# Query heads store both products of the rotation; the key-value norm and the filler sums move with it

## The reference, cut to what matters

```python
proj = jnp.einsum("bsd,dp->bsp", u, w_in)          # q_lat (384), kv_lat (256), k_rope (32), ...
q = rms_norm(q_lat, q_norm_g) @ w_uq               # 8 heads of 64 + 32
q_nope, q_pe = jnp.split(q, [QK_NOPE], axis=-1)
q_pe = apply_rope(q_pe, cos, sin)                  # [x1*cos - x2*sin, x2*cos + x1*sin]
kv = rms_norm(kv_lat, kv_norm_g) @ w_ukv           # 8 heads of k_nope 64 + v 64
k_pe = apply_rope(k_rope, cos, sin)                # one for all heads
qf = concat(q_nope, q_pe);  kf = concat(k_nope, k_pe)
sc = einsum("bqhd,bkhd->bhqk", qb, k) * scale      # then mask, softmax, times v
```

## Time and profile before

| | us |
|---|---|
| median of 3 runs | 2353.86 |
| lowest, highest | 2351.16, 2355.52 |
| span of the profiled execution, first to last instruction | 2352.3 |
| busy in it: PE, DVE, POOL, ACT | 2254.0, 1487.5, 1082.5, 850.4 |
| mean granted TensorE clock (share of full speed) | 0.988 |

### The profile page before, as it was taken

The page is one execution under the profiler, slowest core; times in us unless marked ns, Lnnn a source line. Parts: engine busy times, 40 slices in busy tenths (PEclk is TensorE's granted clock), DMA queues, the critical chain, the costliest instruction groups (busy, mean ns, idle before and its releaser), DMA issues.

```text
span 2352.3 us, 29969 instructions
## 1 busy us (share of the span) xinstructions
PE 2254.0 (96%) x10766; PEld 1834.4 (78%) x10766; DVE 1487.5 (63%) x2357; ACT 850.4 (36%) x1387; POOL 1082.5 (46%) x1273
## 2 busy tenths in 40 slices
PE   6899999999999999999999999999999999999997
PEld 3688777788668877788867888887877878788886
DVE  5989866554478986765368776555775766533322
ACT  2443334222353333422245434344343444433321
POOL 1565436565446543666534455341444344443343
PEclk9999999999999999999999999999999999999999
DMA  8432224664243221354322223233244242222222
GB/s 307 134 110 82 68 73 143 207 202 156 72 143 108 81 67 59 130 169 149 116 81 73 92 99 104 79 116 119 85 123 138 90 126 77 71 72 72 72 81 72
DMA packets 93204, 259.80 MB, mean 110 GB/s; under 512 B 10129, under 2 KB 11537, under 8 KB 92945
## 3 DMA queue, kind: packets, MB, share of 16 engines
q1 hardware_dynamic: 71392, 210.23, 28.6%
q10 hardware_dynamic: 21680, 47.79, 5.7%
HBM read 237.01 MB, written 20.97 MB: 110 GB/s over the span
## 4 chain that ended last, share of the span: by engine, by line
PE 41%; issue 29%; POOL 19%; DVE 7%; ACT 2%; DMA 1%; POOLq 0%; ACTq 0%; DVEq 0%; SPq 0%
POOL t L422 19%; PE bank L2132 13%; PE bank L2133 13%; PE bank L2134 13%; DVE t L1786 3%; PE bank L2206 1%; DVE t L1224 1%; PE bank L2183 1%; DMA t<-blocks 1%; PE bank L2522 1%; DVE t L1228 0%; PE bank L2225 0%; DVE t L1783 0%; POOL t L432 0%; DVE t L1257 0%
## 5 line engine op out<-in xcount | busy, mean ns | idle before, releaser
L422 POOL TENSOR_TENSOR t<-t,t 128x256 fp32r<-128x256 f32 x1208 | 1030.5, 884 | 1179.4 <-ACT t L485 1178.9
L2132 PE MATMUL bank<-t,t 128*128 128x512 f32 (+1 forms) x3056 | 1175.4, 385 | 32.9 <-DVE t L1224 9.4
L2133 PE MATMUL bank<-t,t 128*128 128x512 f32 (+1 forms) x3056 | 1148.4, 376 | 0.0
L2134 PE MATMUL bank<-t,t 128*128 128x512 f32 (+1 forms) x3056 | 1147.2, 375 | 0.0
L2132 PEld LDWEIGHTS bank<-t,t 128*128 128x128 f32 x3056 | 580.0, 190 | 163.5 <-issue 16.0
L2133 PEld LDWEIGHTS bank<-t,t 128*128 128x128 f32 x3056 | 580.0, 190 | 103.2 <-issue 4.2
L2134 PEld LDWEIGHTS bank<-t,t 128*128 128x128 f32 x3056 | 578.4, 189 | 105.1
L485 ACT ACTIVATE t<-t 128x1024 fp32r<-128x1024 f32 x302 | 317.2, 1054 | 287.5 <-PE bank L2134 240.1
L1288 DVE SCALAR_TENSOR_TENSOR t<-t,t,t 128x512 f32<-128x512 f32 x168 | 156.4, 950 | 101.8 <-DMA t<-w_ada 62.0
L1571 DVE SCALAR_TENSOR_TENSOR t<-t,t,t 128x512 f32<-128x512 f32 x240 | 206.1, 859 | 6.7
L1228 DVE SCALAR_TENSOR_TENSOR t<-t,bank 128x512 f32<-128x512 f32 x112 | 76.7, 685 | 153.3 <-ACT t L1181 59.9
(11 more groups left out here) (251 smaller groups left out, 1731.2 us busy)
## 6 DMA issues: line engine op xcount, KB each, us to landing
t<-blocks SPq DMA_DIRECT2D x306, 512.0 KB, 3.6
t<-w_ada SPq DMA_DIRECT2D x144, 256.0 KB, 2.7
t<-w_ada SPq DMA_DIRECT2D x20, 512.0 KB, 11.6
xm_park<-t ACTq DMA_DIRECT2D x16, 384.0 KB, 2.3
s_park<-t ACTq DMA_DIRECT2D x16, 384.0 KB, 2.3
t<-xm_park ACTq DMA_DIRECT2D x16, 384.0 KB, 4.5
t<-s_park ACTq DMA_DIRECT2D x16, 384.0 KB, 5.0
xc_park<-t ACTq DMA_DIRECT2D x16, 256.0 KB, 2.3
```

The source lines that it names most:

```text
L422: low = pool.tensor_tensor(w_lo[slot][:, part], w_raw[slot][:, part], w_hi[slot][:, part].bitcast(F32), ALU.subtract)
L2132: pe.matmul(out, wh, xh, start=start, stop=False)
L2133: pe.matmul(out, wh, xl, start=False, stop=False)
L2134: return pe.matmul(out, wl, xh, start=False, stop=stop)
```

## The change

- `qf` and `kf` have 128 rows instead of 96. For a query head DVE makes one multiplication over rows 64 to 127 (bank times `rope`), straight into `qf`, with no temporary and no addition. The two products stand as separate rows, and the score's sum over 128 rows adds them; for that the rotated key stands in rows 64 to 95 and again in 96 to 127 of `kf`.
- For the key the two products are made as before; the sum is written twice. PE's head 3, which takes the key's bank, waits for the two products (`k_parts`) instead of for the sum.
- The key-value norm on DVE is placed behind head 0 instead of behind head 1, knH on ACT behind head 3 instead of head 5, knL on DVE behind head 4 instead of head 3.
- The steps of `products` are called behind heads 4 to 7 (`products(B_UQ + h // 2 + 1)`) instead of behind heads 0, 1, 3, 5 and 7. The order on SP, the table `ADA_AT` and the points of `split_to` on ACT stay as they are.
- The four filler sums ahead of head 6 on PE are gone, and the wait for `kv_std` with them.

```diff
-        qf, kf = at(R_Q, [96, HEADS, S]), at(R_Q + 16 * KB, [96, HEADS, S])
+        qf, kf = at(R_Q, [128, HEADS, S]), at(R_Q + 16 * KB, [128, HEADS, S])
...
                     if h in (2, 5):
                         split_to(B_UQ(l) + RING + (h + 1) * 3 // 8)
-                    if h == 5:
+                    if h == 3:
                         for j in range(2):
                             act.wait_ge(dve_done, Dn(l, "kn", j))
...
-                def rotate(dst, bank, *label):
+                def turned_keys(bank):
...
-                    dve.tensor_tensor(dst, tmp[3][64:96, :], tmp[4][64:96, :], ALU.add).then_inc(dve_done, d(*label))
+                    for half in (slice(64, 96), slice(96, 128)):
+                        dve.tensor_tensor(tmp[2][half, :], tmp[3][64:96, :], tmp[4][64:96, :], ALU.add).then_inc(dve_done, d())
+                    cd.also(l, "k_rope")
...
                 for h in range(HEADS):
                     wp(l, "q", h)
-                    rotate(qf[64:96, h, :], banks[Q_BANK[h % 4]], l, "q_pe", h)
+                    dve.tensor_tensor(qf[64:128, h, :], banks[Q_BANK[h % 4]][64:128, :], rope[64:128, :], ALU.mult).then_inc(dve_done, d(l, "q_pe", h))
                     if h == 0:
-                        products(B_UQ(l))
-                    if h == 1:
-                        products(B_UQ(l) + 1)
-
                         wa(l, "kv_std")
...
-                    if h == 3:
+                    if h == 4:
                         for j in range(2):
                             wa(l, "knH", j)
                             low(knL[:, j, :], kv_lat[:, j, :], knH[:, j, :], l, "knL", j)
-                    if h % 2:
+                    if h >= 4:
                         products(B_UQ(l) + h // 2 + 1)
...
-                    if h == 6:
-                        pe.wait_ge(act_done, A(l, "kv_std"))
-                        keep_busy(2, 4)
...
-                        pe.wait_ge(dve_done, Dn(l, "k_rope"))
+                        pe.wait_ge(dve_done, Dn(l, "k_parts"))
```

More of the change, by code:

```diff
@@ L1487, in _ @@
                 products(B_KR(l))
-                def rotate(dst, bank, *label):
+                def turned_keys(bank):
                     wd()
                     dve.tensor_tensor(tmp[3][64:96, :], bank[64:96, :], rope[64:96, :], ALU.mult).then_inc(dve_done, d())
-                    dve.tensor_tensor(tmp[4][64:96, :], bank[96:128, :], rope[96:128, :], ALU.mult).then_inc(dve_done, d())
+                    dve.tensor_tensor(tmp[4][64:96, :], bank[96:128, :], rope[96:128, :], ALU.mult).then_inc(dve_done, d(l, "k_parts"))
                     wd()
-                    dve.tensor_tensor(dst, tmp[3][64:96, :], tmp[4][64:96, :], ALU.add).then_inc(dve_done, d(*label))
+                    for half in (slice(64, 96), slice(96, 128)):
+                        dve.tensor_tensor(tmp[2][half, :], tmp[3][64:96, :], tmp[4][64:96, :], ALU.add).then_inc(dve_done, d())
+                    cd.also(l, "k_rope")
                 wp(l, "k_rope")
-                rotate(tmp[2][64:96, :], banks[1], l, "k_rope")
+                turned_keys(banks[1])
                 for h in range(HEADS):
                     wp(l, "q", h)
-                    rotate(qf[64:96, h, :], banks[Q_BANK[h % 4]], l, "q_pe", h)
+                    dve.tensor_tensor(qf[64:128, h, :], banks[Q_BANK[h % 4]][64:128, :], rope[64:128, :], ALU.mult).then_inc(dve_done, d(l, "q_pe", h))
                     if h == 0:
-                        products(B_UQ(l))
-                    if h == 1:
-                        products(B_UQ(l) + 1)
                         wa(l, "kv_std")
@@ L1517, in _ @@
                             low(knL[:, j, :], kv_lat[:, j, :], knH[:, j, :], l, "knL", j)
-                    if h % 2:
+                    if h >= 4:
                         products(B_UQ(l) + h // 2 + 1)
                 for h in range(HEADS):
-                    dve.tensor_copy(kf[64:96, h, :], tmp[2][64:96, :]).then_inc(dve_done, d(l, "k_pe", h))
+                    dve.tensor_copy(kf[64:128, h, :], tmp[2][64:128, :]).then_inc(dve_done, d(l, "k_pe", h))
                 wp(l, "v", 3)
```

## The result

The changed kernel takes 2358.45 us (median of 13 runs, 2355.62 to 2364.04), the kernel before 2353.26 (median of 13). The ratio is 1.0023, 95% interval 1.0013 to 1.0034: slower by 5.2 us, near the 2359.5 that was forecast. The profiled execution has a span of 2356.7 us against 2352.3.

A forecast was written before the change was run, and what follows sets the result against it. PE, busy 96% of the span, was taken as the bound, paced by DVE's chain around the query heads. Delays 1.6 + 1.3 plus clock 2 x 1.5 make 5.9 us: span 2358.2, median 2359.8, taken as 2359.5; range 2349 to 2366.

The forecast's parts named there:

- block 10 waits in SP's queue behind steps 8 and 9: SP's unchanged queue: block 10's load stands behind the moved steps, so in layer 0 its issue goes from 98.65 to 106.9.
- Layer 0: PE's fourth matmul of key chunk 0 starts at 115.85, 1.6 us later than 114.27, after 6.4 us idle.
- Layer 1: PE's fourth matmul of key chunk 0 starts at 701.85, 1.3 us later than 700.56, after 6.3 us idle.
- POOL's range: Low part of a block on POOL: four pieces take 2.83 to 3.97 us; 3.40 was taken for block 10.
- Clock: PE behind the idle stretch in key chunk 0: half clock for 3 us loses 1.5 us per layer, bounds 0 and about 2.
- The row at 838.98: Profile row taken as agreeing that PE's clock falls after a wait; 663.03 did not agree.
- the block's own delay: Block 10 reaching PE's fourth matmul of chunk 0 later than before: 1.6 us in layer 0, 1.3 in layer 1.
- the 4.9 and 5.0 us that the edit opened: PE would be ready for block 10 earlier, at 109.4 in layer 0 (4.9 us) and 695.55 in layer 1 (5.0 us).
- a shift of this stage reaches the end: From chunk 0's fourth matmul to the branches both kernels do the same work, PE nearly always busy, so shifts reach the end.
- the block is not waited for: Rival: block 10 is there by 109.4 and 695.5, so the 9.9 us gain is realised, 2344 us; 12%.
- the clock is kept: Rival: PE resumes at full clock in one or both layers, or the block lands sooner, 2355 to 2358.5 us; 28%.
- steps 10 to 13 bite too: Rival: their tiles land late or loads of blocks 11 and 12 collide with them, 3 to 8 us more, 2363 to 2368; 10%.

The follow-up runs named there:

- the filler in the wait: The changed kernel with six filler sums added ahead of key chunk 0, where PE idles: 2355.52 us, 1.0008 to the kernel before.
- only the rows: The kernel before with only the query heads' two products kept as separate rows, all places as before: 0.9952 in the first set, 0.9972 in the second.
- the first experiment: The changed kernel with, on SP alone, block 10's load issued ahead of the loads waiting for steps 8 and 9: 2345.97 us, 0.9969 to the kernel before.
- the norm behind head 2: The changed kernel with block 10's load ahead of steps 8 and 9, DVE's norm behind head 2, ACT's rounding of block 10 behind head 3: 2350.13 us.
- the steps back: The changed kernel with steps 8 and 9 on DVE behind head 0 again, ahead of the norm, SP unchanged: 2351.65 us, 0.9988 to the kernel before.

## Why the prediction was right

- **The step that decided it, that block 10 waits in SP's queue behind steps 8 and 9, was right.** Issue, landing and rounding came in that order, and moving the load alone took 12 to 13 us off the changed kernel. It was found by laying the code's order beside 98.24 and 98.65, not by any wait in the profile of before: there was slack, so no row named it.
- **Layer 0.** Worked out: fourth matmul of chunk 0 later by 1.6 us. Measured from the key's products: 114.27 - 91.84 = 22.43 before, 117.84 - 93.87 = 23.97 after, so 1.5. Inside it terms were off and cancelled, which is luck: the two scalings took 2.48 us instead of 1.41, so head 1 came 1.3 us later than before and not 0.2; steps 8 and 9 took 1.3 us in all instead of 2.1, and POOL 3.21 instead of 3.40. The later head 1 also held PE back, so that its wait for block 10 was 5.00 us and not 6.4.
- **Layer 1.** Worked out: 1.3 us later. Measured from the sums of squares: 23.79 before, 23.63 after, so 0.2 earlier. This part of the sum was wrong, even in its sign; the wait, 4.71 us instead of 6.3, was there all the same. The three terms of it: POOL 2.76 us instead of 3.40, the landing 3.8 (697.62 to 701.40) instead of 4.1, the steps 1.4 us to SP's next issue (695.82 to 697.25) instead of 1.8. The low end of POOL's range, 2.83, to which the rule of the Trainium skill (GPSIMD Engine Reference, Specifications) on the shared interface had pointed, was the right one here: DVE waits for tiles meanwhile.
- **Clock.** Worked out: 1.5 us per layer. From the fourth matmul to the values: 119.96 - 114.27 = 5.69 before and 125.23 - 117.84 = 7.39 after in layer 0, so 1.7 us; in layer 1 29.48 - 23.79 and 30.93 - 23.63, so 1.6. The row at 838.98 was the right neighbour. With the filler in the wait, the loss is gone.
- **Sum.** Stages 5.9 us worked out, 4.7 measured; the runs gave 5.2. The two halves did not fare alike: the block's own delay was put at 2.9 us and measured 1.4, the clock was put at 3.0 and measured 3.3. So most of the loss is the low clock behind the wait; the delay of the block only eats up the 4.9 and 5.0 us that the edit opened. That a shift of this stage reaches the end holds to within 4 us for nine of the ten experiments, which is loose beside effects of 5 us (stages against runs: -8.9 and -7.3, -3.2 and -2.8, +1.3 and +1.9, -5.0 and -4.0, +3.8 and +4.0, -5.1 and -6.6, +0.6 and -1.4, -12.3 and -8.5, +19.6 and +21.7, the runs by their ratios); the first set of only the rows, -5.0 and -11.3, is the exception. The signs agree in all but the smallest, +0.6 and -1.4.
- **The rivals.** That the block is not waited for fell in the first experiment. That the clock is kept was wrong in both layers. That steps 10 to 13 bite too was right as a danger and did not happen in the changed kernel; it did with the norm behind head 2, once the rest was earlier.

## What to carry to other kernels

The lesson is about order. Before moving work on one engine, list which loads in another engine's queue wait for it and what stands behind them in that queue, even if nobody uses the moved result soon. Slack in such a load shows as nothing at all in a profile; compare its issue time with the end of the work ahead of it. Filler on an idle TensorE is not free to remove: here its four sums were worth 4 us in clock, and they should move to where the wait moves (six of them there gave back 3.4 us by the stages).

## What had not been expected of the hardware

- The same instructions change in length with their neighbours. The four pieces of a low part took 2.76 to 3.98 us in these stages of the two kernels; and the two scalings of the norm, 1.41 us before, took 2.48 when they ran beside such a low part. POOL in layer 0 of the changed kernel, beside the scalings at 100.87 on DVE:

```profile
100.93 3.69 POOL L432 TENSOR_TENSOR t<-t,t 128x256 fp32r<-128x256 f32 x4
```

  Running side by side does not slow DVE every time: with the steps back, the eight copies of the key took 2.79 us although a low part of POOL started 1.14 us into them, at 118.68, and it was the low part that took long, 4.34 us. What decides which of the two gives way is open:

```profile
117.54 2.79 DVE L1522 COPY t<-t 64x512 f32<-64x512 f32 x8
```

- One multiplication over 64 partitions takes the 0.69 us of one over 32.
- After 1.97 us of idle the clock fell, before head 5, in both profiles; after the 1.13 us of the earlier trace rows it did not, nor after the 2.69 us of the earlier trace rows. The length of the idle stretch alone did not decide it.
